# Attention scores of a streaming encoder step: shorter mask additions, one block-diagonal matmul for the sampled queries, one values matmul for two query blocks

## Chip, cores and metric

The kernel runs on one core of one Trainium2 chip. The metric is the device time of one launch in microseconds. The kernel before took 956.37 us (median of 3 runs, 956.13 to 960.84).

## The reference, cut to what matters

Two layers (`DEPTH = 2`) of a hybrid encoder work on 256 prompt tokens and 64 sampled tokens, with a model width of 1024. The part that the change touches is the attention of both branches:

```python
# branch A (8 query heads, 2 key heads, head_dim 64): block-causal window of chunks of 64
s = einsum(q, k) * SCALE;  s = where(chunk of key in [chunk of query - 2, chunk of query], s, NEG)
p = sink_softmax(s, sink);  o = p @ v
# branch B (8 heads): strictly causal, with decay
s = einsum(q, k) * SCALE + F[t] - F[s];  s = where(kpos <= qpos, s, NEG)
p = softmax(s);  o = p @ v
# sampled tokens: 64 queries against 64 own keys and 128 cached keys
#   branch A: no mask;  branch B: the same sum with F and the causal mask
```

With 256 tokens and chunks of 64, a query of the first block of 128 may see keys only up to its own chunk, and one of the second block sees all keys from two chunks before its own. For branch A the window therefore excludes something only in keys 64 to 127 for the first block, and in keys 0 to 63 and 192 to 255 for the second. For branch B the causal mask excludes something only in the diagonal blocks of 128 keys. For the sampled queries of branch B it excludes something only among their own 64 keys, and all queries see the 128 cached ones.

The rest of a layer is matmuls of all 320 tokens with the weights `w_in`, `w_pa`, `w_pb`, `w_o`, `w_gate`, `w_up` and `w_down`.

## The kernel before, in words

**Units.** Activations lie transposed, features on partitions and the 320 tokens on the free axis. Every block of weights that gives 128 output features is a unit: 119 places in `UNITS` per layer, in a fixed order: forget, ka, va, four qa, four kb, a gap, four vb, four qb, sixteen gate units, then the output and the feed-forward units. SyncE loads a unit's weights into one of four slots of `raw` (L549). ScalarE rounds them to fp32r (`w_hi`, L972), VectorE subtracts to get the rest (`w_lo`, L1226), and TensorE makes three matmuls of 320 columns for each 128 rows of weights (L676 to L678). ScalarE and VectorE work three units ahead (`AHEAD = 3`).

**Order of the work between the units.** `SCHEDULE` hangs steps on units, and each engine walks through units and steps in that order. The eight pairs of heads (`PAIRS = 8`; pairs 0 to 3 are branch A, which the code calls swa, pairs 4 to 7 branch B, which it calls fox) come at units 8, 11, 14, ..., 29. For pair p, `scores` and `soften` (normalising) stand after unit 8+3p, `turn` (the transposes of the probabilities) after unit 10+3p, `values` after unit 12+3p. Each of these steps on TensorE stands between the matmuls of two units. The steps share PSUM banks 4 to 7 in turn, in the order of `USES`; `claim` waits until the use four places before is read out. For a pair that order is s2, s0, s1 (sampled, head 0, head 1), then t0, t1, t2, then o.

**Scores on TensorE (L842 to L882).** Head 0 of a pair has its queries and keys on partitions 0 to 63, head 1 on 64 to 127. Each head gets one matmul for the first query block (128 keys, L860) and one for the second (256 keys, L863), so each uses 64 rows and 128 columns of the array. The sampled queries (64 of them, 192 keys, L867) take 64 rows and 64 columns for each head, and both heads write one bank. In branch B two bf16 matmuls follow on that bank, L870 for the decay `F` and L872 for the mask, on all 192 columns. Last, for each head, comes in branch B a bf16 matmul of 384 columns for the decay (L880) and in both branches one of 384 columns that adds the mask from the table `cb` (L882): the identity `id16` is the stationary operand, the mask the moving one.

**Softmax.** VectorE takes the row maxima (L1456), ScalarE the exponentials (L1089), VectorE normalises (L1473), TensorE transposes (L746), ScalarE and VectorE copy to `probs_t` (L1101, L1104, L1480).

**Values on TensorE (L884 to L910).** Five steps for each head of a pair, each step a matmul with 64 stationary columns of `kv` or `vcache` and probabilities as the moving operand. The first two steps have the same stationary block `kv[:, 0, v]`, once for query block 0 and once for query block 1, of 128 columns each.

**Where the queries come from.** `qT` holds the scaled queries of all pairs, for all 320 tokens. In branch A ScalarE copies them (L990) and VectorE rotates them (`rope`, L1440 to L1442; i = 0 are the keys, i = 1 to 4 the query pairs). In branch B ScalarE's copy at L990 is all.

**Start.** VectorE makes six memsets (L1551 to L1556) that each raise `set_once`; ScalarE waits for all six before its first copy (L1165, L1167).

Of the kernel before, what the change touches and what calls it, by code (L numbers as in the profile page):

```python
# [29 lines left out]
P = 128  # L30
F32, F32R, BF16 = mybir.dt.float32, mybir.dt.float32r, mybir.dt.bfloat16
ALU = mybir.AluOpType
ACT = mybir.ActivationFunctionType
# [3 lines left out]
DM, TP, TS, DEPTH, PAST = 1024, 256, 64, 2, 128  # L37
HD, DFF, CONV = 64, 2816, 3
CHUNK = 64
ALPHA = (2.0 * DEPTH) ** 0.25  # L40
SCALE = HD ** -0.5
# [3 lines left out]
TOK = TP + TS  # L45
KC = DM // P
FT = DFF // P
KEYS = TOK + PAST
# [192 lines left out]
def build(nc, A, O):  # L241
# [3 lines left out]
    with ExitStack() as ctx:  # L245
        def sb(name, shape, dt=F32):
            return ctx.enter_context(nc.sbuf_tensor(name, shape, dt))
# [24 lines left out]
        qT = within("qT", 2 * PAIRS * TOK, [P, PAIRS, TOK])  # L272
# [33 lines left out]
        roped_a = sb("roped_a", [P, TOK])  # L306
        roped_b = sb("roped_b", [P, TOK])

        probs = sb("probs", [P, 2, 960])
        probs_t = sb("probs_t", [P, 3, 3 * P])  # L310
        nmax = sb("nmax", [P, PAIRS, 5])
# [332 lines left out]
        def _(pe):  # L644
            def claim(l, key):

                at = USE[key]  # L650
                back = at - 4
                while back >= 0 and USES[back] is None:
                    back -= 4
                if back >= 0:
                    pe.wait_ge(*released(l, USES[back]))
                elif at < 3:
                    pe.wait_ge(var_ready, n(l, 2, 2))
                return bank[4 + at % 4]
# [80 lines left out]
            def done(mm):  # L739
                mm.then_inc(spare_done, 1)  # L740
# [101 lines left out]
            def scores(l, p):  # L842

                fox = p >= 4
                pe.wait_ge(masks_ready, 1)
                if fox:
                    pe.wait_ge(f_ready, n(l, 1, 1))
                    pe.wait_ge(copied, n(l, COPIED[("qb", p - 4)], N_COPIED))
                else:
                    pe.wait_ge(roped, n(l, p + 2, 5))  # L850
                k = kT[:, p - 3, :] if fox else kT[:, 0, :]
                mask = CB_FOX if fox else CB_SWA
                outs = []
                for hd in range(2):
                    outs.append(claim(l, (f"s{hd}", p)))


                for hd, b in enumerate(outs):
                    rows = slice(hd * HD, (hd + 1) * HD)
                    pe.matmul(b[:, 0:P], qT[rows, p, 0:P], k[rows, 0:P], start=True, stop=False)  # L860
                for hd, b in enumerate(outs):
                    rows = slice(hd * HD, (hd + 1) * HD)
                    pe.matmul(b[:, P:3 * P], qT[rows, p, P:TP], k[rows, 0:TP], start=False, stop=False)  # L863
                own = claim(l, ("s2", p))
                for hd in range(2):
                    rows = slice(hd * HD, (hd + 1) * HD)
                    sampled = pe.matmul(own[rows, 0:TS + PAST], qT[rows, p, TP:TOK], k[rows, TP:KEYS],  # L867
                                        start=True, stop=not fox)
                if fox:
                    pe.matmul(own[:, 0:TS + PAST], cb[0:72, CB_SELS + (p - 4) * P:CB_SELS + (p - 3) * P],  # L870
                              fparts[:, 3 * P:3 * P + TS + PAST], start=False, stop=False)
                    sampled = pe.matmul(own[:, 0:TS + PAST], id16, cb[:, CB_SMP:CB_SMP + TS + PAST], start=False,  # L872
                                        stop=True)
                done(sampled)
                for hd, b in enumerate(outs):
                    if fox:


                        h = 2 * (p - 4) + hd
                        pe.matmul(b[:, 0:3 * P], cb[0:72, CB_SEL + h * P:CB_SEL + (h + 1) * P], fparts[:, 0:3 * P],  # L880
                                  start=False, stop=False)
                    done(pe.matmul(b[:, 0:3 * P], id16, cb[:, mask:mask + 3 * P], start=False, stop=True))  # L882

            def values(l, p):  # L884

                fox = p >= 4
                pe.wait_ge(vcache_in, 32 * n(l, 1, 1))
                pe.wait_ge(first_rows_in, 32 * n(l, 1, 1))
                pe.wait_ge(kv_turned, n(l, values_count(6 + p - 4) if fox else 1, 5))
                pe.wait_ge(turned_act, n(l, 2 * p + 2, 2 * PAIRS))  # L890
                pe.wait_ge(turned_dve, n(l, p + 1, PAIRS))
                b = claim(l, ("o", p))
                f = 6 + p - 4 if fox else 1


                steps = [(lambda v, vc: kv[:, 0, v], lambda hd: probs_t[:, hd, 0:P], 0, P, True, True),
                         (lambda v, vc: kv[:, 0, v], lambda hd: probs_t[:, hd, P:2 * P], P, TP, False, False),
                         (lambda v, vc: kv[:, 1, v], lambda hd: probs_t[:, hd, 2 * P:3 * P], P, TP, False, True),
                         (lambda v, vc: kv[0:SPAN, 2, v], lambda hd: probs_t[0:SPAN, 2, hd * TS:(hd + 1) * TS],
                          TP, TOK, False, False),  # L900
                         (lambda v, vc: vcache[0:SPAN, vc],
                          lambda hd: probs_t[0:SPAN, 2, P + hd * TS:P + (hd + 1) * TS], TP, TOK, False, True)]
                for values_of, probs_of, c0, c1, start, stop in steps:
                    for hd in range(2):
                        v = slice(f * P + hd * HD, f * P + (hd + 1) * HD)
                        rows = slice(hd * HD, (hd + 1) * HD)
                        vc = slice((p - 3) * P + hd * HD, (p - 3) * P + (hd + 1) * HD) if fox else rows
                        mm = pe.matmul(b[rows, c0:c1], values_of(v, vc), probs_of(hd), start=start, stop=stop,  # L908
                                       skip_group_check=True)
                done(mm)  # L910
# [39 lines left out]
        def _(act):  # L950
# [28 lines left out]
            def after(l, u):  # L979
# [6 lines left out]
                elif kind in ("qa", "qb"):  # L986
                    b = tile_wait(l, (kind, i))
                    if kind == "qa":
                        swap(l, i + 1, b, SCALE)
                    sc.activation(qT[:, i + (4 if kind == "qb" else 0), :], b[:, 0:TOK], ACT.Copy,  # L990
                                  scale=SCALE).then_inc(copied, 1)
                elif kind == "kb":
                    b = tile_wait(l, (kind, i))
                    sc.copy(kT[:, 1 + i, 0:TOK], b[:, 0:TOK]).then_inc(copied, 1)
# [167 lines left out]
                    sc.activation(y_out(2, half), y_tile(2, half), ACT.Identity, bias=y_bias[0:TS, :],  # L1162
                                  scale=y_rstd[0:TS, 2:3]).then_inc(y_scaled, 1)

            act.wait_ge(set_once, 6)  # L1165

            sc.copy(warm[:], eps_t[:])  # L1167
            for o in range(1, KC, 2):
# [34 lines left out]
        def _(dve):  # L1203
# [175 lines left out]
            def step(l, kind, i):  # L1379
# [52 lines left out]
                elif kind == "rope":  # L1432
# [6 lines left out]
                    dve.wait_ge(tables_in, 16)  # L1439
                    ve.tensor_tensor(roped_b[:], sin, swapped[:, i % 3, :], ALU.mult)  # L1440
                    link(ve.tensor_tensor(roped_a[:], x, cos, ALU.mult))
                    ve.tensor_tensor(out, roped_a[:], roped_b[:], ALU.add).then_inc(roped, 1)  # L1442
                elif kind == "kv":
                    b, v = spare(l, ("kv", i))
                    dve.wait_ge(spare_done, v)
# [106 lines left out]
            ve.memset(ones8[:], 1.0).then_inc(set_once, 1)  # L1552
            ve.memset(fparts[:], 0.0).then_inc(set_once, 1)
            ve.memset(eps_t[:], EPS).then_inc(set_once, 1)
            ve.memset(stage[:, :, TOK:TURN], 0.0).then_inc(set_once, 1)
            ve.memset(w_hi[:, 0, :, :].bitcast(F32), 0.0).then_inc(set_once, 1)  # L1556

# [66 lines left out]
```

## Time and profile before

| | |
|---|---|
| median of 3 runs | 956.37 us |
| lowest, highest | 956.13 us, 960.84 us |
| profiled execution | 958.38 us, its span 956.6 us |
| granted TensorE clock, mean | 0.990 |
| TensorE busy | 925.4 us (97% of the span), 6470 matmul records |
| VectorE busy | 597.8 us (62%) |
| ScalarE busy | 497.5 us (52%) |
| DMA, mean | 140 GB/s |

PE is TensorE's matmul, PEld its weight load, DVE is VectorE, ACT is ScalarE. An fp32 matmul is carried out in passes and leaves two matmul records with two weight loads; a bf16 or fp32r matmul leaves one of each. The duration of a matmul record runs to a modelled end that overlaps the next ones, so the time that a matmul takes in a row of matmuls is read from the distance of two starts. Matmuls of the two heads that start within some nanoseconds of each other run side by side in two halves of the array.

### The profile page before, as it was taken

The page shows a single profiled execution, that of the slowest core. Times are in us where ns is not written, and L with a number is a line of the kernel's source. Part 1 is how long each engine was busy: PE and PEld are TensorE (multiplying, and loading weights), DVE is VectorE, ACT ScalarE, POOL GpSimd, SP SyncE. Part 2 cuts the span into 40 slices and gives each one's busy share as a digit, 9 for nine tenths or more (in the row PEclk, how much of TensorE's full clock was granted, in tenths as well). Part 3 has the DMA queues.
Part 4 walks back from the last instruction along what each step waited for, and adds up shares of the span by engine and source line. Part 5 has one row for each costly group of instructions (what it writes and reads, how often), then busy time and mean ns, then how long its engine had stood idle before and what let it go on. Part 6 is the DMA issues. An engine that isn't in the chain of part 4 may idle for free.

```text
span 956.6 us, 16348 instructions
## 1 busy us (share of the span) xinstructions
PE 925.4 (97%) x6470; PEld 895.9 (94%) x6470; DVE 597.8 (62%) x1210; ACT 497.5 (52%) x945; POOL 27.8 (3%) x43
## 2 busy tenths in 40 slices
PE   7999999999999999999989999999989999999994
PEld 5989999998999999999989999899989999999994
DVE  4775654578876666545487664448777666655444
ACT  4864554435855556533388545445467555554220
POOL 2000000000000000000000000000000000000002
PEclk9999999999999999999999999999999999999998
DMA  9745434454365455445734453345527455456421
GB/s 265 187 130 143 111 89 132 136 151 133 105 179 162 138 155 152 142 143 157 171 85 127 119 164 104 95 133 155 145 58 223 135 155 154 143 151 192 141 80 56
DMA packets 258053, 133.97 MB, mean 140 GB/s; under 512 B 22486, under 2 KB 254938, under 8 KB 257850
## 3 DMA queue, kind: packets, MB, share of 16 engines
q1 hardware_dynamic: 256218, 127.84, 47.8%
q0 software_dynamic: 1760, 5.09, 1.5%
q8 instruction: 52, 0.85, 0.4%
q14 instruction: 23, 0.19, 0.1%
HBM read 128.47 MB, written 4.57 MB: 139 GB/s over the span
## 4 chain that ended last, share of the span: by engine, by line
PE 96%; DVE 2%; ACT 1%; DMA 0%; issue 0%; SPq 0%; DVEq 0%
PE bank L676 28%; PE bank L677 27%; PE bank L678 27%; PE bank L746 3%; PE bank L908 2%; PE bank L692 1%; PE bank L698 1%; PE bank L695 1%; PE bank L867 1%; PE bank L863 1%; PE bank L860 1%; DVE roped_b L1504 1%; PE bank L882 1%; DVE raw L1268 0%; DMA gates<-in_x_sample 0%; ACT probs L1089 0%
## 5 line engine op out<-in xcount | busy, mean ns | idle before, releaser
L676 PE MATMUL bank<-act_hi,w_hi 128*128 128x320 f32 x1312 | 411.7, 314 | 0.0
L677 PE MATMUL bank<-act_lo,w_hi 128*128 128x320 f32 x1312 | 405.6, 309 | 0.0
L678 PE MATMUL bank<-act_hi,w_lo 128*128 128x320 f32 x1312 | 405.4, 309 | 0.0
L1226 DVE TENSOR_TENSOR w_lo<-raw,w_hi 128x1024 fp32r<-128x1024 f32 (+1 forms) x236 | 283.9, 1204 | 110.2 <-ACT w_hi L972 109.8
L972 ACT CAST w_hi<-raw 128x1024 fp32r<-128x1024 f32 (+1 forms) x236 | 244.2, 1035 | 162.2 <-PE bank L678 154.5
L676 PEld LDWEIGHTS bank<-act_hi,w_hi 128*128 128x128 f32 x1312 | 246.5, 188 | 2.7 <-DVE w_lo L1226 0.3
L677 PEld LDWEIGHTS bank<-act_lo,w_hi 128*128 128x128 f32 x1312 | 246.6, 188 | 0.2
L678 PEld LDWEIGHTS bank<-act_hi,w_lo 128*128 128x128 f32 x1312 | 246.5, 188 | 0.0
L676 PE MATMUL bank<-h_hi,w_hi 128*128 128x320 f32 x352 | 109.7, 312 | 0.0
L678 PE MATMUL bank<-h_hi,w_lo 128*128 128x320 f32 x352 | 108.8, 309 | 0.0
L677 PE MATMUL bank<-h_lo,w_hi 128*128 128x320 f32 x352 | 108.8, 309 | 0.0
L1303 DVE COPY tails<-a_ext 128x2 f32<-128x2 f32 x88 | 10.5, 165 | 90.3 <-ACT conv L1022 90.3
L676 PEld LDWEIGHTS bank<-h_hi,w_hi 128*128 128x128 f32 x352 | 66.1, 188 | 0.1
L677 PEld LDWEIGHTS bank<-h_lo,w_hi 128*128 128x128 f32 x352 | 66.1, 188 | 0.1
L678 PEld LDWEIGHTS bank<-h_hi,w_lo 128*128 128x128 f32 x352 | 66.1, 188 | 0.0
L1016 ACT COPY a_ext<-bank 128x256 f32<-128x256 f32 x44 | 16.4, 372 | 95.0 <-PE bank L678 89.8
L1089 ACT ACTIVATE probs<-bank,nmax 128x128 f32<-128x128 f32 (+2 forms) x80 | 32.5, 421 | 46.0 <-DVE nmax L1456 23.6
L1009 ACT ACTIVATE gates<-bank 128x320 f32<-128x320 f32 x32 | 14.2, 444 | 54.0 <-PE bank L678 54.0
L676 PE MATMUL bank<-o_hi,w_hi 128*128 128x320 f32 x128 | 39.6, 309 | 0.0
L677 PE MATMUL bank<-o_lo,w_hi 128*128 128x320 f32 x128 | 39.6, 309 | 0.0
L678 PE MATMUL bank<-o_hi,w_lo 128*128 128x320 f32 x128 | 39.6, 309 | 0.0
L1456 DVE TENSOR_REDUCE nmax<-bank 128x1 f32<-128x128 f32 (+2 forms) x80 | 22.6, 350 | 25.1 <-PE bank L882 25.1
(204 smaller groups left out, 971.4 us busy)
## 6 DMA issues: line engine op xcount, KB each, us to landing
raw<-in_w_in SPq DMA_DIRECT2D x62, 512.0 KB, 3.9
raw<-in_w_gate SPq DMA_DIRECT2D x44, 512.0 KB, 3.8
raw<-in_w_up SPq DMA_DIRECT2D x44, 512.0 KB, 4.3
raw<-in_w_down SPq DMA_DIRECT2D x32, 448.0 KB, 3.8
raw<-in_w_o SPq DMA_DIRECT2D x16, 512.0 KB, 3.9
raw<-in_w_down SPq DMA_DIRECT2D x16, 512.0 KB, 4.1
raw<-in_w_in SPq DMA_DIRECT2D x16, 256.0 KB, 5.5
raw<-in_w_pa SPq DMA_DIRECT2D x32, 128.0 KB, 2.9
```

Source lines behind the costliest of these rows:

```text
L676: pe.matmul(out, wh, hi[:, k0 + c, :], start=begin and c == 0, stop=False)
L677: pe.matmul(out, wh, lo[:, k0 + c, :], start=False, stop=False)
L678: mm = pe.matmul(out, wl, hi[:, k0 + c, :], start=False, stop=end and c == n_chunks - 1)
L746: return pe.transpose(out, src, id32[0:rows, 0:rows])
L908: mm = pe.matmul(b[rows, c0:c1], values_of(v, vc), probs_of(hd), start=start, stop=stop, skip_group_check=True)
L972: sc.copy(w_hi[:, slot, :, :].rearrange("p c e -> p (c e)")[:, 0:w], raw[:, slot, 0:w]).then_inc(hi_made, credit(u))
L1009: sc.activation(gates[:, i + (KC if kind == "gb" else 0), :], b[:, 0:TOK], ACT.Tanh, scale=0.5).then_inc(copied, 1)
L1016: sc.copy(e[:, 2:2 + TP], b[:, 0:TP])
L1089: ins = sc.activation(pr[:, at:at + w], src, ACT.Exp, bias=nmax[:, i, g:g + 1], accum_out=den[:, i, g:g + 1])
L1226: ve.tensor_tensor(w_lo[:, slot, :, :].rearrange("p c e -> p (c e)")[:, 0:w], raw[:, slot, 0:w], hi.bitcast(F32), ALU.subtract).then_inc(l ...
L1303: ve.tensor_copy(tails[:].rearrange("p (s r j) -> p s r j", s=2, r=2)[:, s, :, i], e[:, last:last + 2]).then_inc(tail_copied, 1)
L1456: ins = ve.tensor_reduce(nmax[:, i, g:g + 1], b[:, c0:c0 + w], AX.X, ALU.max, negate=True)
```

## The change

- **Masks.** `masked(of)` picks 256 of the 384 columns: in branch B column blocks 0 and 2, in branch A two pieces of 128 columns that begin at columns 64 and 256. The mask matmul moves before the decay matmul of branch B. The sampled mask of branch B is added on the 64 own keys in place of 192, and also moves before the decay.
- **Sampled queries.** A new tile `q_own` (128 x 4 x 128, fp32) holds for each of four pairs a 128 x 128 block with head 0's queries in the upper left and head 1's in the lower right, zeros elsewhere. One fp32 matmul with 128 rows and 128 columns replaces the two of 64 by 64. It stands between the two heads' first-block matmuls and their second-block matmuls.
- **Writing `q_own`.** In `rope`, VectorE's last addition over 320 columns becomes three: 256 columns, and one 64 x 64 block for each head. In branch B, ScalarE's copy of 320 columns becomes one of 256 columns and two of 64 x 64.
- **Start.** A seventh memset sets `q_own` to zero.
- **Values.** The first block's matmul takes both query blocks, 256 columns, in place of two of 128.

```diff
+        q_own = sb("q_own", [P, 4, P])
...
+                def masked(of):
+
+                    if fox:
+                        return of[:, 0:3 * P].rearrange("p (k c) -> p k c", c=P)[:, 0:3:2, :]
+                    return of[:, HD:HD + 3 * P].rearrange("p (k c) -> p k c", k=2)[:, :, 0:P]
+
+                def add_mask(b):
+                    return pe.matmul(masked(b), id16, masked(cb[:, mask:]), start=False, stop=not fox)
 
                 for hd, b in enumerate(outs):
                     rows = slice(hd * HD, (hd + 1) * HD)
                     pe.matmul(b[:, 0:P], qT[rows, p, 0:P], k[rows, 0:P], start=True, stop=False)
+                own = claim(l, ("s2", p))
+                sampled = pe.matmul(own[:, 0:TS + PAST], q_own[:, p % 4, :], k[:, TP:KEYS], start=True, stop=not fox)
                 for hd, b in enumerate(outs):
                     rows = slice(hd * HD, (hd + 1) * HD)
                     pe.matmul(b[:, P:3 * P], qT[rows, p, P:TP], k[rows, 0:TP], start=False, stop=False)
-                own = claim(l, ("s2", p))
-                for hd in range(2):
-                    rows = slice(hd * HD, (hd + 1) * HD)
-                    sampled = pe.matmul(own[rows, 0:TS + PAST], qT[rows, p, TP:TOK], k[rows, TP:KEYS],
-                                        start=True, stop=not fox)
                 if fox:
-                    pe.matmul(own[:, 0:TS + PAST], cb[0:72, CB_SELS + (p - 4) * P:CB_SELS + (p - 3) * P],
-                              fparts[:, 3 * P:3 * P + TS + PAST], start=False, stop=False)
-                    sampled = pe.matmul(own[:, 0:TS + PAST], id16, cb[:, CB_SMP:CB_SMP + TS + PAST], start=False,
-                                        stop=True)
+
+                    pe.matmul(own[:, 0:TS], id16, cb[:, CB_SMP:CB_SMP + TS], start=False, stop=False)
+                    sampled = pe.matmul(own[:, 0:TS + PAST], cb[0:72, CB_SELS + (p - 4) * P:CB_SELS + (p - 3) * P],
+                                        fparts[:, 3 * P:3 * P + TS + PAST], start=False, stop=True)
                 done(sampled)
                 for hd, b in enumerate(outs):
+                    mm = add_mask(b)
                     if fox:
-
-
                         h = 2 * (p - 4) + hd
-                        pe.matmul(b[:, 0:3 * P], cb[0:72, CB_SEL + h * P:CB_SEL + (h + 1) * P], fparts[:, 0:3 * P],
-                                  start=False, stop=False)
-                    done(pe.matmul(b[:, 0:3 * P], id16, cb[:, mask:mask + 3 * P], start=False, stop=True))
+                        mm = pe.matmul(b[:, 0:3 * P], cb[0:72, CB_SEL + h * P:CB_SEL + (h + 1) * P],
+                                       fparts[:, 0:3 * P], start=False, stop=True)
+                    done(mm)
...
-                steps = [(lambda v, vc: kv[:, 0, v], lambda hd: probs_t[:, hd, 0:P], 0, P, True, True),
-                         (lambda v, vc: kv[:, 0, v], lambda hd: probs_t[:, hd, P:2 * P], P, TP, False, False),
+                steps = [(lambda v, vc: kv[:, 0, v], lambda hd: probs_t[:, hd, 0:2 * P], 0, TP, True, False),
...
-                    sc.activation(qT[:, i + (4 if kind == "qb" else 0), :], b[:, 0:TOK], ACT.Copy,
-                                  scale=SCALE).then_inc(copied, 1)
+                    if kind == "qa":
+                        sc.activation(qT[:, i, :], b[:, 0:TOK], ACT.Copy, scale=SCALE).then_inc(copied, 1)
+                    else:
+                        sc.activation(qT[:, i + 4, 0:TP], b[:, 0:TP], ACT.Copy, scale=SCALE)
+                        for hd in range(2):
+                            rows = slice(hd * HD, (hd + 1) * HD)
+                            ins = sc.activation(q_own[rows, i, rows], b[rows, TP:TOK], ACT.Copy, scale=SCALE)
+                        ins.then_inc(copied, 1)
...
-            act.wait_ge(set_once, 6)
+            act.wait_ge(set_once, 7)
...
-                    ve.tensor_tensor(out, roped_a[:], roped_b[:], ALU.add).then_inc(roped, 1)
+                    if i == 0:
+                        ve.tensor_tensor(out, roped_a[:], roped_b[:], ALU.add).then_inc(roped, 1)
+                    else:
+                        ve.tensor_tensor(out[:, 0:TP], roped_a[:, 0:TP], roped_b[:, 0:TP], ALU.add)
+                        for hd in range(2):
+                            rows = slice(hd * HD, (hd + 1) * HD)
+                            ins = ve.tensor_tensor(q_own[rows, i - 1, rows], roped_a[rows, TP:TOK],
+                                                   roped_b[rows, TP:TOK], ALU.add)
+                        ins.then_inc(roped, 1)
...
+            ve.memset(q_own[:], 0.0).then_inc(set_once, 1)
```

## Rows read from the trace of the kernel before

**Rows 1.** The page's chain by engine, and one row of TensorE's waits.

```profile
PE 96%; DVE 2%; ACT 1%; DMA 0%; issue 0%; SPq 0%; DVEq 0%
...
PE bank L860 <- ACT probs_t L1104: 1.0, 2, 0.5
```

**Rows 2.** Timeline of TensorE's matmuls, pair 0, layer 0: start us, length us.

```profile
48.68 0.31 PE L678 MATMUL bank<-act_hi,w_lo 128*128 128x320 f32 x1
48.92 0.49 PE L860 MATMUL bank<-kT,qT 64*128 64x128 f32 x4
49.24 0.60 PE L863 MATMUL bank<-kT,qT 64*128 64x256 f32 x4
49.77 0.54 PE L867 MATMUL bank<-kT,qT 64*64 64x192 f32 x4
50.25 0.50 PE L882 MATMUL bank<-cb 128*128 128x384 bf16 x2
50.45 0.45 PE L676 MATMUL bank<-act_hi,w_hi 128*128 128x320 f32 x1
50.73 0.31 PE L677 MATMUL bank<-act_lo,w_hi 128*128 128x320 f32 x1
```

**Rows 3.** The same timeline in narrower windows, where second passes stand alone.

```profile
49.46 0.38 PE L863 MATMUL bank<-kT,qT 64*128 64x256 f32 x2
...
49.99 0.33 PE L867 MATMUL bank<-kT,qT 64*64 64x192 f32 x2
```

**Rows 4.** Timeline of TensorE's weight loads in the same stretch, idle time in brackets.

```profile
48.92 0.30 PEld L860 LDWEIGHTS bank<-kT,qT 64*128 64x128 f32 x4 [0.19 <-issue]
...
49.77 0.19 PEld L867 LDWEIGHTS bank<-kT,qT 64*64 64x64 f32 x4 [0.33 <-issue]
50.24 0.11 PEld L882 LDWEIGHTS bank<-cb 128*128 128x128 bf16 x2 [0.28 <-issue]
```

**Rows 5.** Timeline of TensorE's matmuls, pair 6 (branch B), layer 1.

```profile
600.04 0.31 PE L678 MATMUL bank<-act_hi,w_lo 128*128 128x320 f32 x1
...
601.70 0.25 PE L872 MATMUL bank<-cb 128*128 128x192 bf16 x1
601.79 0.33 PE L880 MATMUL bank<-fparts,cb 72*128 72x384 bf16 x1
601.96 0.33 PE L882 MATMUL bank<-cb 128*128 128x384 bf16 x1
...
602.60 0.31 PE L677 MATMUL bank<-act_lo,w_hi 128*128 128x320 f32 x1
```

**Rows 6.** Timeline of TensorE's matmuls in values, pair 0, layer 0.

```profile
65.08 0.99 PE L908 MATMUL bank<-probs_t,kv 128*64 128x128 f32 x16
65.90 0.29 PE L908 MATMUL bank<-probs_t,vcache 96*64 96x64 f32 x4
```

**Rows 7.** Groups by line and form, weight loads: busy us, mean ns, idle before.

```profile
L676 PEld LDWEIGHTS bank<-act_hi,w_hi 128*128 128x128 f32 x1312 | 246.5, 188 | 2.7 <-DVE w_lo L1226 0.3
...
L867 PEld LDWEIGHTS bank<-kT,qT 64*64 64x64 f32 x64 | 3.1, 131 | 5.3 <-issue 5.3
```

**Rows 8.** Timeline of the start: weight loads of the input transposes, and VectorE.

```profile
6.76 0.59 PEld L746 LDWEIGHTS bank<-cf,gates 64*128 64x128 f32 x3 [0.33 <-issue]
...
2.14 0.91 DVE L1556 MEMSET w_hi<- 128x1024 f32 x1 [0.16 <-issue]
7.17 0.49 DVE L1561 COPY xT<-bank 128x320 f32<-128x320 f32 x1 [4.11 <-PE bank L746]
```

**Rows 9.** Groups by line and form: the two writers of the queries.

```profile
L1442 DVE TENSOR_TENSOR qT<-roped_a,roped_b 128x320 f32<-128x320 f32 x8 | 3.9, 493 | 0.3
...
L990 ACT ACTIVATE qT<-bank 128x320 f32<-128x320 f32 x16 | 7.1, 441 | 12.8 <-PE bank L678 12.7
```

**Rows 10.** Timeline between normalising and transposing, pair 0, layer 0.

```profile
55.22 1.24 DVE L1473 TENSOR_SCALAR probs<-probs,rden 128x128 f32<-128x128 f32 x5
...
58.24 1.03 PE L746 MATMUL bank<-cf,probs 128*128 128x128 f32 x8
```

## The prediction

> **What bounds the kernel now.** I began with the chain that ended last: 96% of it is TensorE [rows 1]. TensorE's waits come next. The only one inside the attention is 1.0 us before L860, at two places [rows 1]. It is pair 1's, which follows straight on pair 0's transposes in each layer and waits for their copies. The third view is the weight loads by form: for all 1312 loads of L676, late weights (`w_lo`) cost 0.3 us in the whole run [rows 7]. So ScalarE, VectorE and the DMAs are covered. A nanosecond more or less of TensorE's own work between two units is one of the end time, and little else counts. The timeline of a scores block then shows what it is made of. A branch A block lies between the starts of L678 at 48.68 and L677 at 50.73, 2.05 us with two ordinary matmuls in it [rows 2]; a branch B block from 600.04 to 602.60, 2.56 us [rows 5]. There are 8 of each (2 layers, 4 pairs).
>
> The reader should see the steps in which this block is *not* streaming. L863's two heads run side by side, their first passes at 49.24 and their second at 49.46 [rows 2, 3]: a pass of 256 columns takes 0.22 us, 0.86 ns per column. The second should be streamed at 49.68. But the weights for L867 start to load only at 49.77, after 0.33 us without any load [rows 4]. Between weights of one shape the loads run ahead under the matmuls (L863's first loads stand within L860's); here they did not. What changes there is the piece of the array: 64 rows by 128 columns, then 64 by 64. The same stands ahead of L860 (0.19 us without a load) and ahead of L882 (0.28 us) [rows 4]. So each change of shape costs about 49.77 - 49.68 = 0.09 us of emptying, and then the first load, which nothing hides.
> That first load: L867's second passes start at 49.99; a pass of 192 columns is 192 x 0.86 = 0.165 us, so the first really began near 49.83, 0.055 us after the load began, for 64 columns of weights. For 128 columns I take twice that, 0.11 us. The lengths of the two forms, 188 and 131 ns, differ by the same 0.057 us [rows 7].
>
> **The change part by part.**
> 1. *Masks on 256 columns.* The price of bf16 columns: L880, 384 columns, takes 601.96 - 601.79 = 0.17 us; L872, 192 columns, 601.79 - 601.70 = 0.09 us [rows 5]. The 192 columns between them cost 0.08 us, 0.42 ns each; 128 columns are 0.053 us. Two heads, 16 pairs: -1.7 us, all on TensorE's path. Moving the mask before the decay matmul alters nothing: both are 128-column bf16 matmuls on the same bank.
> 2. *Sampled mask on 64 columns*, branch B only: -0.053 us, 8 times, -0.4 us. No row has a bf16 matmul of 64 columns. The bounds are no gain at all (it stays at L872's 0.09) and that full gain; I take the gain, since 0.42 ns a column held from 384 to 192.
> 3. *One block-diagonal matmul in place of two.* The two were side by side already, so halving the instructions halves nothing: two passes of 192 columns before, two after. The weights that are exposed after the change of shape are 128 columns wide in place of 64: +0.057 us, 16 times, +0.9 us. The change of shape ahead of it was there before (64x128 to 64x64) and is there after (64x128 to 128x128).
> 4. *Its new place.* Before, a block changed shape three times: into 64x128, to 64x64, to 128x128. Now it is 64x128 (L860), 128x128 (`q_own`), 64x128 again (L863), 128x128 (masks): four times. The added one stands before L863 and costs 0.09 us plus an exposed load of 128 columns, 0.11 us: +0.20 us, 16 times, +3.2 us. Behind it nothing is saved, since in branch A the masks meet a change as before, and in branch B the change merely moves from before L870 to before the first mask matmul. The step that moves also claims bank s2 earlier, by L863's 0.5 us. Its bank's last reader is four uses back, for most pairs the previous pair's exponentials or values, long over. For pair 1, L860 has already waited for the later copies.
> 5. *Values.* L908 has 16 records from 65.08 to 65.90 [rows 6], in pairs side by side: six passes of 128 columns and two of 64, so with 0.86 ns per column 0.66 + 0.11 = 0.77 us of the 0.82. The columns are the same after; the loads saved were hidden under them. L863's 256 columns at 0.86 ns are no cheaper per column than these. I take 0. Bounds: nothing, and the surplus 0.05 us once in 16 blocks, -0.8 us.
> 6. *Writers of `q_own`.* VectorE makes three additions for one, eight times (four pairs, two layers); none is longer than L1442's 493 ns [rows 9], so at most 0.99 us more each. ScalarE makes three copies for one of 441 ns [rows 9], at most 0.88 us more, eight times. What hides them is the lead of three units: weights came late by 0.3 us in all [rows 7], and after pair 0's normalising, which ends at 55.22 + 1.24 = 56.46, TensorE begins the transposes only at 58.24 [rows 10]. If that cover were gone, all 16 would cost at most 15 us. But 1 us of delay does not use up a lead of three units, 72 ordinary matmuls. Taken as 0.
> 7. *The memset.* 128x1024 took 0.91 us [rows 8], so 128x512 about half. VectorE then stands idle 4.11 us until TensorE's first transposes at 7.17 [rows 8], and ScalarE has nothing to do before them either: 0. Without that cover, 0.5 us.
>
> Sum. Branch A: -0.106 + 0.057 + 0.20 = +0.15 us per block, +1.2 for eight. Branch B: 0.053 less, +0.10 per block, +0.8. In all **+2.0 us**. The profiled execution took 958.38 us (span 956.6), so its like would take 960.4; the median of the runs was 956.37, 2.0 below it, and I set the forecast against that: **958.4 us**. No stall elsewhere is lengthened: the block's first mask is finished some 0.2 us later within it, against the 1.8 us between normalising and transposes [rows 10].
>
> The changes of shape are the term that decides the sign. The row shows a load that begins 0.09 us after the previous matmul's last column. The Trainium skill, page "TensorEngine Tiling (Array Packing)", section "Tiling Modes", says it so: "Changing tiling mode (not just tile) drains the TensorE". By that rule the added change is paid in full, and the trace agrees for the three changes that it has.
>
> **The rivals.**
> *A. Only a change in columns drains.* Then going from 64 to 128 rows at 128 columns, and back, is free. The kernel before never does it in this block except on entering (128x128 to L860), and there 0.19 us without a load speak against it [rows 4]; in the start's transposes, 64x128 between 128x128, the loads stop for 0.33 us each time at the low clock [rows 8]. For it: the entry also has a wait. The 3.2 us of part 4 vanish: -1.2 us, **955.2 us**.
> *B. The array empties, but the load runs meanwhile.* Loads that meet other rows, or a spare copy of the weights, could start under the running matmul. Then 0.11 us of the added change goes, 16 times: +2.0 - 1.8 = +0.2 us, **956.6 us**. Against it, L867's load shows 0.33 us without a load and begins after the end of L863 [rows 4]. The Trainium skill, page "TensorE: Matmul & The Clock Gate", section "Part 2: What happens when you issue a matmul", has such a rule: TensorE pulls a weight load ahead when row groups don't conflict or it goes to the background buffer. The trace shows it inside a shape, and not across one.
> *C. Slower: columns in two pieces stream at half speed.* The mask matmul L882 now reads and writes two separate runs of 128 columns. No row before has that form. If each column cost 0.84 ns in place of 0.42, a mask would take 0.107 us more, 32 times, +3.4 us on top of the 2.0: **961.8 us**. It decides from a mask matmul of about 0.2 us. Against it: the columns are still read in order within each piece, 128 at a time.
> *D. The late copies.* The extra work of part 6 delays a `w_lo`. It would show as TensorE waiting at L676; no row has a lead under a unit's length, and I leave it within the rest.
>
> **How the numbers follow.** Forecast (+2.0 us) 0.70, A 0.14, B 0.10, C 0.04, others 0.02. A measurement of this kernel can tell about 0.5% from no change, that is 4.8 us: 951.6 to 961.2. The forecast, A and B all lie inside; C lies outside, above; others are split. Faster 0.01, the same 0.94, slower 0.05. The range: parts 2 and 5 give 957.6 to 958.8 about the forecast; it reaches down to A, 955.2, and upwards takes in half of C's surcharge, 1.7 us: 955.1 to 960.2.
>
> **What would show each step.** Right: in the timeline, L863's first load begins about 0.09 us after the `q_own` matmul's last column, with idle time beside it; a branch A block of 2.20 us and a branch B block of 2.66 between the same ordinary matmuls; masks at 0.11 us each; `q_own` passes 0.165 us apart; values unchanged at 0.82 us up to the `vcache` matmuls. Wrong: loads without a gap around `q_own` (A), a gap without an exposed load (B), masks at 0.2 us (C), idle time of TensorE on `w_lo`, `roped` or `copied` (D). A result outside 955.1 to 960.2, or a block of branch A that got shorter, would refute the argument.

## The result and the profile after

| | before | changed |
|---|---|---|
| median of 20 executions | 956.77 us | 960.37 us |
| lowest, highest | 955.73, 960.84 us | 959.48, 962.15 us |
| profiled execution, its span | 958.38, 956.6 us | 960.16, 958.4 us |

The changed kernel takes 1.0028 times the time of the kernel before (95% interval 1.0018 to 1.0038), which is 1.7 to 3.6 us more. The forecast was +2.0 us, 958.4 us by the first median. By the ratio that median of 956.37 becomes 959.0 us, within the range of 955.1 to 960.2; the changed kernel's own median, 960.37, lies just above it. The interval includes the 2.0 us; the medians themselves are 3.6 us apart, and the difference is taken up below.

First the block of pair 0, layer 0, in the timeline of the changed kernel's matmuls (start us, length us), to be held against [rows 2]:

```profile
47.89 0.31 PE L679 MATMUL bank<-act_hi,w_lo 128*128 128x320 f32 x1
48.13 0.49 PE L869 MATMUL bank<-kT,qT 64*128 64x128 f32 x4
48.55 0.59 PE L871 MATMUL bank<-kT,q_own 128*128 128x192 f32 x2
49.08 0.70 PE L874 MATMUL bank<-kT,qT 64*128 64x256 f32 x4
49.71 0.39 PE L865 MATMUL bank<-cb 128*128 128x256 bf16 x2
49.86 0.39 PE L677 MATMUL bank<-act_hi,w_hi 128*128 128x320 f32 x1
50.09 0.30 PE L678 MATMUL bank<-act_lo,w_hi 128*128 128x320 f32 x1
```

From the last ordinary matmul's start to the second next one's it is 50.09 - 47.89 = 2.20 us, where it was 2.05. The weight loads of the same stretch, to be held against [rows 4]:

```profile
48.13 0.30 PEld L869 LDWEIGHTS bank<-kT,qT 64*128 64x128 f32 x4 [0.19 <-issue]
48.55 0.30 PEld L871 LDWEIGHTS bank<-kT,q_own 128*128 128x128 f32 x2
49.07 0.30 PEld L874 LDWEIGHTS bank<-kT,qT 64*128 64x128 f32 x4 [0.23 <-issue]
49.71 0.11 PEld L865 LDWEIGHTS bank<-cb 128*128 128x128 bf16 x2 [0.33 <-issue]
```

The 0.23 us before L874 did not exist: there L863 followed L860 with its loads hidden. The change ahead of L871, in rows alone, has a gap too: L869's loads end at 48.13 + 0.30 = 48.43, 0.12 us before L871's first one (the view prints idle time only above 0.15 us). A block of branch B, pair 6 of layer 1, to be held against [rows 5]:

```profile
602.93 0.31 PE L679 MATMUL bank<-act_hi,w_lo 128*128 128x320 f32 x1
...
604.75 0.20 PE L877 MATMUL bank<-cb 128*128 128x64 bf16 x1
604.78 0.25 PE L878 MATMUL bank<-fparts,cb 72*128 72x192 bf16 x1
604.87 0.27 PE L865 MATMUL bank<-cb 128*128 128x256 bf16 x1
604.98 0.33 PE L885 MATMUL bank<-fparts,cb 72*128 72x384 bf16 x1
...
605.57 0.31 PE L678 MATMUL bank<-act_lo,w_hi 128*128 128x320 f32 x1
```

It lasts 605.57 - 602.93 = 2.64 us, where it was 2.56. A mask of 256 columns now takes 604.98 - 604.87 = 0.11 us, and the one of 64 columns 0.03 us.

TensorE's waits show what is new between the blocks. The first row stood at the kernel before as 1.0 us for both places [rows 1]; it is now two rows, one for each layer, and a third is new:

```profile
PE bank L869 <- DVE probs_t L1498: 0.7, 1, 0.7
PE bank L869 <- ACT probs_t L1114: 0.5, 1, 0.5
PE bank L912 <- ACT probs L1099: 0.4, 2, 0.2
```

This table has all scores blocks by the same measure, from the start of the last ordinary matmul ahead of the block to the start of the second one behind it. Pair 1's block also holds pair 0's transposes and the wait for their copies; A is pair 0, B each pair of branch B. Pairs 2 and 3 of branch A are not in the table: their blocks also hold three transposes and last 2.38 us before, 2.52 to 2.53 us changed, so they grew by the same 0.14 to 0.15 us. The prediction counts them as blocks of 2.05 us, which doesn't alter its sum. The sums are over all 16 scores blocks and the 16 stretches with values, against the kernel before.

| kernel | A, pair 0 | A, pair 1, layers 0 / 1 | B | sum, us |
|---|---|---|---|---|
| before | 2.052 | 3.521 / 3.522 | 2.558 | 0 |
| changed | 2.199 | 3.665 / 3.885 | 2.646 | +2.1 |
| changed, again | 2.198 | 3.665 / 3.835 | 2.646 | +2.0 |
| masks_only | 1.948 | 3.419 / 3.460 | 2.449 | -1.5 |
| pair_middle | 2.251 | 3.723 / 3.722 | 2.751 | +3.1 |
| writers_only | 2.052 | 3.519 / 3.950 | 2.558 | +0.4 |
| values_only | 2.051 | 3.522 / 3.518 | 2.559 | -0.1 |
| own_last | 1.896 | 3.360 / 3.875 | 2.340 | -2.5 |
| own_first | 1.801 | 3.017 / 3.547 | 2.248 | -4.4 |
| own_first_turn | 1.802 | 2.940 / 2.939 | 2.249 | -5.1 |

### The profile page after: what moved, and what is told of

Read it like the earlier page. It is cut to its first block, busy times and chain, and to the rows that moved or that the text cites. A ratio compares the mean times of both kernels' runs of the same rounds, so it can differ in the third digit from the quotient of the medians.

```text
span 958.4 us, 16189 instructions
## 1 busy us (share of the span) xinstructions
PE 927.0 (97%) x6374; PEld 895.7 (93%) x6374; DVE 600.5 (63%) x1227; ACT 499.9 (52%) x961; POOL 27.8 (3%) x43
## 4 chain that ended last, share of the span: by engine, by line
PE 92%; DVE 3%; ACT 3%; issue 1%; DMA 0%; SPq 0%; DVEq 0%
PE bank L677 27%; PE bank L679 26%; PE bank L678 26%; PE bank L747 3%; PE bank L912 2%; PE bank L693 1%; PE bank L699 1%; PE bank L696 1%; PE bank L874 1%; PE bank L871 1%; ACT w_hi L976 1%; PE bank L869 1%; DVE roped_b L1522 1%; ACT probs L1052 1%; ACT probs L1099 1%
## 5 line engine op out<-in xcount | busy, mean ns | idle before, releaser
L677 PE MATMUL bank<-act_hi,w_hi 128*128 128x320 f32 x1312 | 411.2, 313 | 0.0
L677 PEld LDWEIGHTS bank<-act_hi,w_hi 128*128 128x128 f32 x1312 | 246.4, 188 | 1.9 <-DVE w_lo L1236 0.3
L677 PE MATMUL bank<-h_hi,w_hi 128*128 128x320 f32 x352 | 109.7, 312 | 0.0
L677 PEld LDWEIGHTS bank<-h_hi,w_hi 128*128 128x128 f32 x352 | 66.1, 188 | 0.1
L677 PE MATMUL bank<-o_hi,w_hi 128*128 128x320 f32 x128 | 39.6, 309 | 0.0
L1474 DVE TENSOR_REDUCE nmax<-bank 128x1 f32<-128x128 f32 (+2 forms) x80 | 22.6, 349 | 27.0 <-PE bank L885 22.1
```

The costliest lines, as they stand in the source:

```text
L677: pe.matmul(out, wh, hi[:, k0 + c, :], start=begin and c == 0, stop=False)
L1474: ins = ve.tensor_reduce(nmax[:, i, g:g + 1], b[:, c0:c0 + w], AX.X, ALU.max, negate=True)
```

## The experiments

The theory: a change of the array's shape, rows or columns, costs 0.09 us of emptying and a weight load that nothing hides; the change added one in each block. The rivals: A, rows alone don't count; B, no exposed load; C, slow masks in two pieces; and after the result a fourth, that VectorE's and ScalarE's new work costs the rest.

**after_again.** The changed kernel, no edit.

> The changed kernel again, for the size of its loss and as the neighbour of the next three. Theory (the added change of shape costs 0.20 us in 16 blocks): a branch A scores block of 2.20 us and a branch B block of 2.65 us, against 2.05 and 2.56 before, and 2 us more in all. Rival (the work of VectorE and ScalarE for q_own, or something outside the blocks, costs too): the difference of the medians stays near 3.6 us, and 1 us or more of it is outside the blocks.

Measured: 960.60 us median of 12 against 959.00 of 30, ratio 1.0020 (1.0008 to 1.0032). The blocks are those of the changed kernel's first trace within 0.05 us. Its profiled execution took 960.41 us, 2.03 more than the profiled one of before, and its blocks sum to +2.0. So almost nothing of that pair's difference lies outside the attention; the rival's 1 us doesn't appear. In the first trace of the changed kernel it is 1.8 us between the profiled executions and +2.1 in the blocks.

**masks_only.** On the kernel before, with the change's `masked`, whose definition is left out here:

```diff
-                    done(pe.matmul(b[:, 0:3 * P], id16, cb[:, mask:mask + 3 * P], start=False, stop=True))
+                    done(pe.matmul(masked(b), id16, masked(cb[:, mask:]), start=False, stop=True))
```

> The kernel before with only the shorter mask matmuls of the two heads (256 columns in two pieces in place of 384). Theory: 0.053 us less for each of 32 masks, blocks of 1.95 us (A) and 2.45 us (B), 1.7 us faster than before. Rival C (two pieces stream at half speed): blocks of 2.16 us (A) and 2.67 us (B), 1.7 us slower.

Measured: 956.41 us, ratio 0.9984 (0.9971 to 0.9998). That is 0.2 to 2.8 us less by the interval. The blocks shrank by 0.104 and 0.109 us, 0.052 and 0.055 us per mask, against 0.053 foretold. So the two pieces stream as fast as one: rival C falls. These are its masks in the timeline of matmuls, pair 0, layer 0; from the first mask's start to L677's it is 49.57 - 49.19 = 0.38 us, where it was 50.73 - 50.25 = 0.48 [rows 2]:

```profile
49.19 0.39 PE L887 MATMUL bank<-cb 128*128 128x256 bf16 x2
49.34 0.39 PE L676 MATMUL bank<-act_hi,w_hi 128*128 128x320 f32 x1
49.57 0.31 PE L677 MATMUL bank<-act_lo,w_hi 128*128 128x320 f32 x1
```

**pair_middle.** On the kernel before, the sampled queries' two 64 x 64 matmuls between the two loops, so that a change of shape is added and nothing else is touched:

```diff
+                own = claim(l, ("s2", p))
+                for hd in range(2):
+                    ...
+                    sampled = pe.matmul(own[rows, 0:TS + PAST], qT[rows, p, TP:TOK], k[rows, TP:KEYS],
+                                        start=True, stop=not fox)
                 for hd, b in enumerate(outs):
                     rows = slice(hd * HD, (hd + 1) * HD)
                     pe.matmul(b[:, P:3 * P], qT[rows, p, P:TP], k[rows, 0:TP], start=False, stop=False)
-                own = claim(l, ("s2", p))
-                ...
```

> The kernel before with only the place of the sampled queries' two 64x64 matmuls changed: between the heads' first-block and second-block matmuls. It makes an added change of shape without q_own and without shorter masks. Theory: L863 gets an exposed load of 128 columns and the emptying before it, +0.20 us in each of 16 blocks: 2.25 us (A) and 2.76 us (B) against 2.05 and 2.56, 3.2 us slower than before. Rival (the added time of the changed kernel lies in the wide q_own load and not in the place): blocks as before within 0.05 us, 0 us.

Measured: 963.20 us against 956.55, ratio 1.0058 (1.0040 to 1.0077). The blocks grew by 0.199 and 0.193 us, +3.1 us in all: the place alone gives the whole added term. Its weight loads, where before L863's followed L860's without a gap:

```profile
49.77 0.20 PEld L864 LDWEIGHTS bank<-kT,qT 64*64 64x64 f32 x4
50.24 0.30 PEld L868 LDWEIGHTS bank<-kT,qT 64*128 64x128 f32 x4 [0.28 <-issue]
50.87 0.11 PEld L882 LDWEIGHTS bank<-cb 128*128 128x128 bf16 x2 [0.33 <-issue]
```

The ratio's point estimate is 5.5 us, 2.4 more than the blocks' sum, and even its lower end (+3.8 us) lies above it. The last section comes back to that.

**own_last.** On the changed kernel, the `q_own` matmul behind both second-block matmuls:

```diff
-                own = claim(l, ("s2", p))
-                sampled = pe.matmul(own[:, 0:TS + PAST], q_own[:, p % 4, :], k[:, TP:KEYS], start=True, stop=not fox)
                 for hd, b in enumerate(outs):
                     rows = slice(hd * HD, (hd + 1) * HD)
                     pe.matmul(b[:, P:3 * P], qT[rows, p, P:TP], k[rows, 0:TP], start=False, stop=False)
+                own = claim(l, ("s2", p))
+                sampled = pe.matmul(own[:, 0:TS + PAST], q_own[:, p % 4, :], k[:, TP:KEYS], start=True, stop=not fox)
```

> The changed kernel with the q_own matmul behind both heads' second-block matmuls, where the sampled queries stood before. Then the array changes shape twice in a block (into 64x128, into 128x128), as q_own and the masks have one shape. Theory (each change is about 0.09 us of emptying and an exposed load, 0.11 us for fp32 and 0.02 us for bf16): blocks of 1.89 us (A) and 2.34 us (B), 5.0 us faster than the changed kernel and 3.0 us faster than the kernel before: 953.8 us where before is 956.8. Rival A (only a change of columns empties the array): no faster than the changed kernel by more than 0.5 us, since no columns change in either. Rival B (emptying but no exposed load): 1.6 us less gain than the theory.

Measured: 955.83 us, ratio 0.9978 (0.9962 to 0.9993), 0.7 to 3.6 us faster than the kernel before; 3.0 us were foretold, and the blocks give 2.5. Blocks of 1.896 and 2.340 us against 1.89 and 2.34 foretold. Between this kernel and the changed one no shape differs in its columns alone, all have 128, and yet each block but pair 1's of layer 1 is 0.30 us shorter: rival A falls. Rival B falls too: it had foretold a gain 0.1 us smaller in each block, and the gain is the full one. The loads show the masks' first load inside the q_own matmul, with no idle time, since they share a shape (it begins at 49.94, and the q_own loads end at 49.66 + 0.30 = 49.96):

```profile
49.66 0.30 PEld L874 LDWEIGHTS bank<-kT,q_own 128*128 128x128 f32 x2 [0.33 <-issue]
49.94 0.26 PEld L865 LDWEIGHTS bank<-cb 128*128 128x128 bf16 x2
```

Pair 1 of layer 1 stayed long, 3.875 us against 3.360 in layer 0. That was not foretold, and two more kernels deal with it below.

**own_first.** On the changed kernel, `q_own` and in branch B its two bf16 matmuls ahead of the claims of the heads' banks, behind the unit's 128 x 128 matmuls:

```diff
+                own = claim(l, ("s2", p))
+                sampled = pe.matmul(own[:, 0:TS + PAST], q_own[:, p % 4, :], k[:, TP:KEYS], start=True, stop=not fox)
+                if fox:
+                    ...
+                done(sampled)
                 outs = []
                 for hd in range(2):
                     outs.append(claim(l, (f"s{hd}", p)))
```

> The changed kernel with the q_own matmul (in branch B with its two bf16 matmuls) ahead of everything else in the block, straight after the unit's matmuls of 128x128. Two changes of shape again, but the q_own load is hidden under the unit's matmuls, and the exposed load before the masks is the short bf16 one. Theory: blocks of 1.80 us (A) and 2.25 us (B), 4.5 us faster than the kernel before, 952.3 us where before is 956.8. Rival A: as the changed kernel. If emptying alone counted and no load, own_first and own_last would be equal; the theory has own_first 1.4 us ahead. In pair 1, which waits for the copies of pair 0's probabilities, the matmul may fill the wait: up to 0.5 us more, twice.

Measured: 954.47 us, ratio 0.9957 (0.9940 to 0.9973). Blocks of 1.801 and 2.248 us against 1.80 and 2.25; in all -4.4 us against -4.5 foretold. The 0.09 us by which it leads own_last in the blocks without a wait is the wide fp32 load, hidden here under a unit, against the short bf16 one: a load is really exposed behind a change of shape. Its loads, pair 0, layer 0:

```profile
48.39 0.34 PEld L855 LDWEIGHTS bank<-kT,q_own 128*128 128x128 f32 x2
48.95 0.30 PEld L877 LDWEIGHTS bank<-kT,qT 64*128 64x128 f32 x4 [0.23 <-issue]
49.17 0.31 PEld L880 LDWEIGHTS bank<-kT,qT 64*128 64x128 f32 x4
49.81 0.11 PEld L873 LDWEIGHTS bank<-cb 128*128 128x128 bf16 x2 [0.33 <-issue]
```

Two changes of shape are left of four, those before L877 and before L873. The loads also answer a rival that the prediction doesn't name, that the gaps are `claim`'s waits for a bank and not the shape's: here a claim stands right before L855, within one shape, and its first load has no idle time before it; the gaps before L873 here and before L874 in the changed kernel have no claim. In layer 0 pair 1's block fell by 0.50 us, 0.25 more than the others: the matmul fills part of the wait for the copies.

**values_only.** The kernel before with only the values change (the diff in the front part). One execution, so no interval.

> The kernel before with only the values change: one matmul of 256 columns for both query blocks. Theory: the weight loads saved were hidden, so a values block between ordinary matmuls stays at 1.53 us (at most 0.01 us less), and the whole gains less than 0.1 us. Rival: each of the two passes saved takes its fixed cost of 0.03 us with it, blocks of 1.47 us, 1 us in all.

Measured: 959.64 us in one execution. The stretch of pair 0 in the timeline of matmuls:

```profile
64.91 0.31 PE L678 MATMUL bank<-act_hi,w_lo 128*128 128x320 f32 x1
65.14 0.99 PE L907 MATMUL bank<-probs_t,kv 128*64 128x256 f32 x12
65.96 0.29 PE L907 MATMUL bank<-probs_t,vcache 96*64 96x64 f32 x4
...
66.43 0.30 PE L677 MATMUL bank<-act_lo,w_hi 128*128 128x320 f32 x1
```

From 65.14 to 65.96 it is 0.82 us as before [rows 6], with 12 records in place of 16. In finer digits a block went from 1.529 to 1.525 us, 0.06 us over all 16. The rival's 0.06 us for each block is not there.

**writers_only.** The kernel before with the tile, its memset and its writers, and no reader:

```diff
+                        sc.activation(qT[:, i + 4, :], b[:, 0:TOK], ACT.Copy, scale=SCALE)
+                        for hd in range(2):
+                            rows = slice(hd * HD, (hd + 1) * HD)
+                            ins = sc.activation(q_own[rows, i, rows], b[rows, TP:TOK], ACT.Copy, scale=SCALE)
...
+                        ve.tensor_tensor(out, roped_a[:], roped_b[:], ALU.add)
+                        for hd in range(2):
+                            rows = slice(hd * HD, (hd + 1) * HD)
+                            ins = ve.tensor_tensor(q_own[rows, i - 1, rows], roped_a[rows, TP:TOK],
+                                                   roped_b[rows, TP:TOK], ALU.add)
```

> The kernel before with the tile q_own, its memset and its writers added (qT's sampled columns still written too, nothing reads q_own). VectorE and ScalarE have the added instructions of the change, TensorE exactly its old ones. Theory as corrected by the trace after the change: only pair 1's block of layer 1 grows, where TensorE waits for VectorE's copy of pair 0's probabilities: 3.52 us before, 3.9 there; all other blocks within 0.01 us; in all 0 to 0.5 us. Rival (the rest of the change's loss beyond the blocks comes from these engines): 1 us or more slower.

Measured: 957.49 us against 956.55, ratio 1.0002 (0.9989 to 1.0015). That is 1.1 us less to 1.4 us more. Fifteen blocks are as before; one, pair 1 of layer 1, grew from 3.522 to 3.950 us, and TensorE's waits name VectorE:

```profile
PE bank L861 <- DVE probs_t L1495: 1.0, 1, 1.0
PE bank L861 <- ACT probs_t L1111: 0.5, 1, 0.5
```

VectorE's timeline in the changed kernel shows how it gets there. In layer 1 the four rotations run late, and the last one stands right before pair 0's maxima (L1474):

```profile
518.19 0.43 DVE L1455 TENSOR_TENSOR qT<-roped_a,roped_b 128x256 f32<-128x256 f32 x1
518.53 0.45 DVE L1458 TENSOR_TENSOR q_own<-roped_a,roped_b 64x64 f32<-64x64 f32 x2
519.00 1.41 DVE L1474 TENSOR_REDUCE nmax<-bank 128x1 f32<-128x128 f32 x5
```

The maxima, a wait for ScalarE's exponentials, the normalising and two `w_lo` of units ahead follow, and then comes the copy for which TensorE waits, without any idle time of VectorE ahead of it:

```profile
524.76 1.22 DVE L1236 TENSOR_TENSOR w_lo<-raw,w_hi 128x1024 fp32r<-128x1024 f32 x1
...
526.05 1.20 DVE L1236 TENSOR_TENSOR w_lo<-raw,w_hi 128x1024 fp32r<-128x1024 f32 x1
527.18 0.54 DVE L1498 COPY probs_t<-bank 128x384 f32<-128x384 f32 x1
```

**own_first_turn.** own_first, and VectorE makes that copy before the second `w_lo`:

```diff
-                    elif UNITS[u + AHEAD] and u not in (0, NORM_UNITS[0], NORM_UNITS[0] + 1):
+                    elif UNITS[u + AHEAD] and u not in (0, 10, NORM_UNITS[0], NORM_UNITS[0] + 1):
                         lo_part(l, u + AHEAD)
...
                         step(l, kind, i)
+                        if u == 10 and kind == "turn":
+                            lo_part(l, u + AHEAD)
```

> The kernel with q_own first, and in addition VectorE copies pair 0's transposed probabilities before it makes the w_lo of three units ahead, not after. Theory: in layer 1 pair 1's block (3.55 us with q_own first, 3.02 in layer 0) falls to 3.0 to 3.1 us, and layer 0's stays; another 0.5 us, 952.0 us where before is 956.8. Rival (the wait is ScalarE's copy): no change in that block. If the w_lo that now comes later is missed, the wait moves to an ordinary unit and nothing is gained.

Measured: 953.22 us against 956.55, ratio 0.9957 (0.9940 to 0.9974). Pair 1's block is 2.940 and 2.939 us in the two layers, 0.61 less than own_first in layer 1 and, not foretold, 0.08 less in layer 0: there, too, own_first's TensorE had waited for VectorE's copy. What is left is a wait for ScalarE's copy, 0.2 us in each layer where the kernel before waited 0.5:

```profile
PE bank L877 <- ACT probs_t L1114: 0.4, 2, 0.2
```

This kernel and own_first beat both kernels of the case. The two have the same ratio; that the second is the faster by 0.7 us is read from the blocks, and the intervals can't tell it; the profiled executions took 953.64 and 953.59 us. Foretold was 4.8 us less than before, the blocks give 5.1, the ratio 4.1 (2.5 to 5.7).

## Why the prediction was right

1. *Masks* (-1.7 us foretold). masks_only: 0.052 to 0.055 us per mask, -1.7 us in the blocks. Pair 1's values take back 0.12: TensorE waits there for ScalarE's exponentials, so that masks_only comes to -1.5.
2. *Sampled mask on 64 columns* (-0.4 us). It takes 0.03 us in place of 0.09, and branch B's block grew by 0.059 us less than A's: the column price holds down to 64 columns, and the choice of the full gain was right.
3. *Wide load of `q_own`* (+0.9 us). Not tried alone. In branch A the changed kernel is pair_middle with masks 0.104 us shorter and `q_own` in place of the pair; its block is 0.052 us shorter, so `q_own` costs 0.052 us a block against 0.057 foretold.
4. *The added change of shape* (+3.2 us). pair_middle: 0.199 and 0.193 us a block against 0.20, +3.1 us. own_last and own_first take changes away and gain what the same two prices, emptying and exposed load, say. The Trainium skill, page "TensorEngine Tiling (Array Packing)", section "Tiling Modes", speaks of a drain at a change of mode. The gaps between weight loads of 0.12 to 0.33 us at each change agree, also where only the number of rows changes.
5. *Values* (0). -0.004 us a block.
6. *Writers* (0). This is the step that failed, by a small amount. Three instructions take 0.42 + 0.45 us where one took 0.49, well below the bound that I gave. The argument was that a lead of three units hides them. It does so for `w_lo`, which was never late. But the lead says nothing of the copies of the transposed probabilities, for which TensorE already waited [rows 1]: the cover there was gone before the change. It cost about 0.2 us in the changed kernel (pair 1: 3.885 and 3.835 in layer 1 against 3.665 in layer 0), 0.4 where the writers stand alone. Some of the 0.2 comes without the writers: in masks_only, too, that block is 0.04 us longer than layer 0's. The 1.8 us between normalising and transposes [rows 10] were those of layer 0, and layer 1 was left unread.
7. *Memset* (0). It took 0.485 us against "about half" of 0.91, and VectorE's idle time before the first input copy became 3.50 us in place of 4.11 [rows 8].

The sum in the blocks is +2.0 to +2.1 us, against +2.0. The new wait of 0.4 us at L912 is before pair 1's values, in both layers, and lengthened their two stretches by only 0.04 us each. masks_only has it too, 0.2 us twice, and pair_middle and writers_only don't, so it came with the shorter masks; that no stall elsewhere is lengthened was not quite true.

What the prediction lacked is a view of how far one execution stands from another: it took the difference of one profiled execution to a median of three as fixed, and the blocks' sum as the medians' difference. Its upper end is 0.1 us off as well, as 958.4 + 1.7 is 960.1. What was foretold and came out is the 2.0 us of the blocks; the 3.6 us between the medians was not foretold.

## What to carry to other kernels

Where TensorE sets the time, count the changes of the array's shape in a stretch before the instructions: matmuls of one shape belong together, and a full 128 x 128 one belongs next to others of that shape. Two matmuls that already run side by side in parts of the array are not made cheaper by merging them into one block-diagonal one; here that was worth it only because it let the sampled queries stand beside the units' or the masks' shape. And a step counted as hidden must be checked at each place where the bound engine already waits, in every layer, not against the average lead.

## What the runs showed of the hardware that was not expected

Outside the attention the time moves with the clock that TensorE is granted around the two normalisations of a layer, and it moves by more than the change. In the 30 executions of before beside the first four experiments, those with a mean granted clock of 0.990 and above took 955.38 to 958.77 us, those with 0.986 or 0.987 took 958.93 to 960.99. Four traces by windows, columns: window, length, then busy us and counts of PE, PEld, DVE, ACT and POOL, granted clock, DMA share, GB/s. Before:

```profile
200.00:280.00 80.00, 77.03 (x507) 75.52 (x506) 62.94 (x124) 47.53 (x84) 2.36 (x4) 0.98 0.47 138
440.00:520.00 80.00, 76.67 (x505) 73.86 (x504) 52.68 (x99) 49.01 (x85) 2.00 (x4) 0.98 0.55 138
680.00:720.00 40.00, 37.04 (x240) 35.90 (x239) 32.35 (x64) 24.10 (x47) 2.36 (x4) 0.96 0.35 99
```

The changed kernel:

```profile
200.00:280.00 80.00, 77.04 (x500) 75.57 (x499) 62.05 (x123) 47.49 (x84) 2.36 (x4) 0.96 0.46 136
440.00:520.00 80.00, 76.67 (x499) 74.23 (x498) 53.22 (x104) 47.59 (x78) 2.00 (x4) 0.96 0.56 139
680.00:720.00 40.00, 37.04 (x246) 35.69 (x245) 32.56 (x61) 23.71 (x47) 1.46 (x3) 1.00 0.33 95
```

The changed kernel again, and pair_middle:

```profile
200.00:280.00 80.00, 77.04 (x509) 75.57 (x508) 63.38 (x124) 47.91 (x85) 2.36 (x4) 0.98 0.47 139
440.00:520.00 80.00, 76.67 (x504) 74.22 (x504) 53.98 (x107) 47.99 (x81) 2.00 (x4) 0.98 0.55 139
```

```profile
200.00:280.00 80.00, 77.04 (x501) 75.57 (x500) 62.23 (x123) 47.38 (x85) 2.36 (x4) 0.96 0.49 141
440.00:520.00 80.00, 76.67 (x501) 74.19 (x500) 52.06 (x94) 48.22 (x80) 2.00 (x4) 0.96 0.54 137
```

The full level is 2.4 GHz and the lower one 1.2 GHz; 0.98 and 0.96 are means over a window in which most of the time was granted the full level and the rest the lower one. TensorE's wait for the activations in these three windows is the same in every trace (5.9 us at three places), and the clock granted beside it is not. Where the grants agree, as in the first and the third, the profiled executions differ by the blocks' sum (2.03 us against 2.0). pair_middle, with less clock in both windows, reached its last ordinary matmuls 5.5 us later than before: 3.1 us in the attention, 0.4 at the start, 2.0 in the rest, which has no changed instruction. writers_only, with a mean clock of 0.993, was 3.0 us *ahead* in that rest.

The rest can be placed. With the ordinary matmuls of each trace set against those of before, one by one, the stretches around the three waits (from 232 to 262, 470 to 500 and 698 to 722 us of before) took 1.1 us more, 0.7 more and 1.2 less in the changed kernel, 1.1, 0.6 and 0.3 more in pair_middle, 1.6, 0.2 and 1.2 less in writers_only. Start, attention and these three stretches together give each trace's distance from before to within 0.11 us. The blocks themselves don't move with the state of the clock: A and B of the table are the same within 0.001 us in writers_only, before and values_only, whose profiled executions took 955.81, 958.38 and 959.64 us. So the 2.0 us in the blocks are firm, and what is open lies in the start and in the grants.

The changed kernel's executions had mean clocks of 0.987 to 0.992, those of before 0.986 to 0.994. Differences in the grants are of the size of the 1.6 us between the medians' difference (3.6) and the blocks' (2.0), and the second measurement of the same two kernels has a medians' difference of 1.6. But the mean clock alone does not explain them. In the second measurement's before, the 14 executions at 0.990 and above have a median of 956.3 us, while the changed kernel's 5 at 0.992 in both measurements took 959.48 to 961.10; the 16 of before at 0.986 and 0.987 have 959.9, and the changed kernel's other 27 about 960.5. Whether the changed kernel meets the lower clock at these three places more often than the one before, or only did in these executions, stays open: its 32 executions include none under 959.48 us, while those of before fall into two groups, and no run here separated the two.
